# GpSimd's weight sums gated on VectorE's, oldest PSUM banks first, and one operand sum moved in an eight-core encoder block

## The chip, the cores and the metric

The kernel runs on the 8 cores of one Trainium2 chip as one program, each core on its own 1024 tokens. Nothing is exchanged between cores. The metric is the device time of one execution in microseconds, that of the slowest core. Each core has TensorE (PE, with its weight loads as PEld), VectorE (DVE), ScalarE (ACT), GpSimd (POOL) and SyncE (SP), each with an instruction queue that runs in order. They are tied together by semaphores.

## What is computed

```python
h = rms_norm(x, norm1_pre)
z = h @ w_in                              # u | v | p | gate_a | gate_b
y_a = sgu_mixer(u, v, ...)                # gMLP mixing in 128-token blocks
y_b = pool_mixer(p, w_pool, scale)        # trailing means, minus the token
merged = sigmoid(z_a) * (y_a @ w_a_out) + sigmoid(z_b) * (y_b @ w_b_out)
x = x + rms_norm(merged @ w_mix_out, norm1_post)
h = rms_norm(x, norm2_pre)
hid = silu(h @ w_gate) * (h @ w_up)
x = x + rms_norm(hid @ w_down, norm2_post)
```

## The kernel before

The whole kernel is a list of operations in program order. `S.add(engine, fn, reads, writes, after)` appends one. Each engine runs its own operations in that order, and waits only for operations of other engines that touch the same memory or stand in `after`. So the order of the Python calls is the order of every queue. The stages are A (input projection, pooling, mixing), B (gates and merge, the "gate stage"), CD (output mix, norms, FFN gate and up) and E (FFN down).

**Seven products for eight.** The gate matrices (stage B, 14 sets j) and the FFN's gate and up matrices (stage CD, 42 sets j) are multiplied by Strassen's scheme in Winograd's form (`Scheme`). A set is a 2x2 of weight quarters, loaded as `raw[j]` by a DMA that GpSimd issues, and it meets the 2x2 of activation quarters h11, h12, h21, h22. A product `prod(j, m)` is 8 matmuls of 128x128 by 128x512 into one PSUM bank. The operands of some products are sums:

- weight sums `wsums(j, part)`, L745: part 0 is s52 (128x2048) and s1 (128x1024) on VectorE, part 1 is s6 and s7 (128x1024 each) on GpSimd. Products 2 and 5 read s52, 1 reads s1, 6 reads s6, 7 reads s7;
- operand sums of the activations, `hsum`, L726 on VectorE, bf16, 4096 columns in the whole form: sums[0] or hs[0] for product 1, sums[1] or hs[1] for product 3, sums[2] or hs[2] for product 4, then h12 and h21 are overwritten by sums, for products 6 and 7.

`add2` (L721) evicts a bank on VectorE, with one input in PSUM and one in SBUF. `copy_out` (L765) evicts one on ScalarE.

**Banks.** `nb()` takes the 8 PSUM banks in rotation. It serves stage A. `balloc()` takes, of the free banks, the one with the smallest `last_use`. At the start of stage B `last_use` is -1 for all, so the first choice is bank 0, whatever stage A used last.

**The start of stage B** (L920 to L940). `gates0(0)` and `gates0(1)` are 8 banks of 16 plain matmuls each (L876), with the operands normalised beside them (L864, two SBUF inputs). `wsums(0, 0)` and `wsums(0, 1)` follow, then sums[1], then `y_part(0)`: 8 banks of 8 matmuls (L907), each evicted by `add2`, and after each pair a sum into `mergedT` (L915, two SBUF inputs). Then sums[2], sums[0], and the first `run_one_set`, which runs products 2, 5, 3, 4, 1, 6, 7 on TensorE and, through `early()`, puts s52 of set 1 and the sums for products 6 and 7 on VectorE.

**The start of the FFN** (L1104 to L1124). After the last token block's norm (L1008 on VectorE) the queue of VectorE holds: part 0 of set 0, hs[2], part 0 of set 1, the product of `d_classic(0, 0)` (L1050), three quarters of hs[0] and hs[1], the product of `d_classic(1, 0)`, half of the last block's transposed copy (L1034, `turn(7)`), the last quarters of hs[0] and hs[1], two more products, and the sums for products 6 and 7. TensorE runs `d_classic(0, 0)` and `(1, 0)` (L1062, 64 matmuls), `turn(7)` (L1027), `start(0)` and `start(1)` (products 2 and 4 of sets 0 and 1), `d_classic(0, 1)` and `(1, 1)` (64 matmuls), then `run(0)` to `run(41)` in the order 2, 3, 5, 1, 4, 6, 7. `d_classic(., 1)` needs both halves of `turn(7)`'s copy. GpSimd's `wsums(0, 1)` waits for L1008 by `after`. GpSimd's queue then has the load of `raw[2]`, and in each `run(j)` the load of set j+3 and `wsums(j + 1, 1)`.

Of the kernel before, what the change touches and what calls it, by code (L numbers as in the profile page):

```python
# [11 lines left out]
ALU = mybir.AluOpType  # L12
# [180 lines left out]
def build_program():  # L193
# [28 lines left out]
    with contextlib.ExitStack() as es:  # L222
        arena_t = es.enter_context(nc.sbuf_tensor("arena", [128, ARENA_BYTES], U8))
        psum_t = es.enter_context(nc.psum_tensor("psum", [128, 8, 512], F32))
        S = Sched(nc)
# [497 lines left out]

        def hsum(out, a_, b_, op, c0, c1):
            o, x_, y_ = out[:, :, c0:c1], a_[:, :, c0:c1], b_[:, :, c0:c1]
            S.add("dve", lambda e: e.tensor_tensor(out=o, in0=x_, in1=y_, op=op), reads=[x_, y_], writes=[o])  # L726

        class Scheme:
            def __init__(self, n, raw, ws, quads, sums, tset, load, outp):
                self.n, self.raw, self.ws, self.tset, self.load, self.outp = n, raw, ws, tset, load, outp  # L730
                (h11, h12), (h21, h22) = quads
                self.x = {1: sums[0], 2: h11, 3: sums[1], 4: sums[2], 5: h22, 6: h12, 7: h21}
                self.held = {}

            def wsums(self, j, part, which=(0, 1), after=()):
                if j >= self.n:
                    return
                r = self.raw[j % len(self.raw)]
                s52, s1, s6, s7 = self.ws[j % len(self.ws)]
                a11, a12, a21, a22 = r[:, 0, 0], r[:, 0, 1], r[:, 1, 0], r[:, 1, 1]  # L740
                jobs = (((s52, r[:, :, 0], r[:, :, 1], ALU.add), (s1, a11, a22, ALU.add)),
                        ((s6, a21, a11, ALU.subtract), (s7, a12, a22, ALU.subtract)))[part]
                for o, x_, y_, op in [jobs[i] for i in which]:
                    S.add("pool" if part else "dve",
                          lambda e, o=o, x_=x_, y_=y_, op=op: e.tensor_tensor(out=o, in0=x_, in1=y_, op=op),  # L745
                          reads=[x_, y_], writes=[o], after=after)

            def prod(self, j, m):
                r = self.raw[j % len(self.raw)]
# [89 lines left out]
        def stage_B():  # L839
# [52 lines left out]
                if d < 16:  # L892
                    dma("pool", wab_slot(d), w_ab[d])

            def y_part(p):
                t_ = (tmp[0] if p else tmp[2], tmp[1])
                for n_, i in enumerate((0, 1, 3, 2) if p < 7 else (1, 0, 2, 3)):
                    f_, hf = place[i]
                    d = 2 * p + f_
                    tk = slice(hf * HT, (hf + 1) * HT)  # L900
                    for q, src in ((0, yAT), (1, ybT)):
                        b = balloc()

                        def mmy(e, b=b, q=q, src=src, d=d, tk=tk):
                            ins = None
                            for kc in range(8):
                                ins = e.matmul(PS(b), lhsT=wab_slot(d)[:, 8 * q + kc, :], rhs=src[:, kc, tk],  # L907
                                               start=(kc == 0), stop=(kc == 7))
                            return ins
                        S.add("pe", mmy, reads=[wab_slot(d), src[:, :, tk]], writes=[PS(b)])  # L910
                        add2(t_[q][i], PS(b), t_[q][i], ALU.mult)
                        bfree(b)
                    a_, b_ = (t_[q][i].rearrange("p (t n) -> p t n", t=4) for q in range(2))
                    dstm = mergedT[:, hf * 4:(hf + 1) * 4, d, :]
                    S.add("dve", lambda e, a_=a_, b_=b_, dd=dstm: e.tensor_tensor(out=dd, in0=a_, in1=b_, op=ALU.add),  # L915
                          reads=[a_, b_], writes=[dstm])
                    if n_ >= 2:
                        wab_load(d + 2)

            wab_load(0)  # L920
            wab_load(1)
            dma("pool", wmix[0], w_mix[0])
# [2 lines left out]
            scheme.wsums(0, 0)  # L925
            scheme.wsums(0, 1)
            hsum(sums[1], h12, h22, ALU.subtract, 0, 512)
            y_part(0)
            hsum(sums[2], h21, h11, ALU.subtract, 0, 512)
            hsum(sums[0], h11, h22, ALU.add, 0, 512)  # L930

            def et2_load():
# [18 lines left out]
        def stage_CD():  # L951
# [40 lines left out]
            def c_chain(it):  # L992
# [12 lines left out]
                rstd_ops(it["ssq2"], it["rs2"], 128)  # L1005
                for i in range(2):
                    c_ = slice(i * 1024, (i + 1) * 1024)
                    it["last"] = S.add("dve", lambda e, i=i, c_=c_: e.scalar_tensor_tensor(  # L1008
                        out=it["xb"][:, c_], in0=it["xs"][:, c_], scalar=it["rs2"], in1=g2r[i],
                        op0=ALU.mult, op1=ALU.mult),  # L1010
                        reads=[it["xs"][:, c_], it["rs2"], g2r[i]], writes=[it["xb"][:, c_]])
# [7 lines left out]
            def turn(t, bank):  # L1019
                for kh in range(2):  # L1020
# [9 lines left out]
                    S.add("pe", tr, reads=[xb_, ident], writes=[PS(b)])  # L1030
                    d_ = h2q[kh][1][:, :, (t - 4) * 128:(t - 3) * 128]
                    s_ = PSB(b).rearrange("p (k n) -> p k n", k=8)
                    if kh:
                        S.add("dve", lambda e, d_=d_, s_=s_: e.tensor_copy(out=d_, in_=s_), reads=[PS(b)], writes=[d_])  # L1034
                    else:
                        S.add("act", lambda e, d_=d_, s_=s_: e.activation(out=d_, in_=s_, func=AF.Copy),
# [76 lines left out]
            scheme.start(0)  # L1113
            scheme.start(1)
            hsum(hs[1], h12, h22, ALU.subtract, 384, 512)
            hsum(hs[0], h11, h22, ALU.add, 384, 512)
            d_classic(0, 1)
            d_classic(1, 1)
            hsum(h12, h11, h12, ALU.add, 0, 512)
            hsum(h21, h21, h22, ALU.add, 0, 512)  # L1120
            scheme.wsums(0, 1, after=[items[7]["last"]])
            raw_load(2)
            for j in range(NM):
                scheme.run(j, j > 0)  # L1124
# [236 lines left out]
```

How the kernel before makes its waits and increments, by code:

```python
        def run(engname, e):  # L173
            waited = {}
            for op in per_eng.get(engname, []):
                need = {}
                for d in op.deps:
                    dop = self.ops[d]
                    if need.get(dop.sem, 0) < dop.sigval:
                        need[dop.sem] = dop.sigval
                for s, v in need.items():
                    if waited.get(s, 0) < v:
                        e.wait_ge(semh[s], v)
                        waited[s] = v
                if op.fn is None:
                    continue
                ins = op.fn(e)
                if op.signal:
                    ins.then_inc(semh[op.sem], 16 if op.dma else 1)
```

## Time and profile before

| what | value |
|---|---|
| median of 3 runs | 1499.78 us (1498.06 to 1500.7) |
| profiled execution, its own time | 1496.78 us |
| its span, slowest core (core 4) | 1495.2 us |
| spans of the eight cores | 1491.7 to 1495.2 us |
| PE busy / PEld busy | 1447.8 us (97%) / 667.4 us (45%) |
| DVE, ACT, POOL busy | 902.4, 301.3, 339.5 us |
| stage B on core 4 | 209.5 to 522 us |
| FFN gate and up, from `start(0)` | 646.2 to 1183.2 us |

The profiled execution's own time is 1.6 us above its span, and 3.0 us below the median of the runs. TensorE is the engine whose idle time counts: in most of the span one matmul follows the other. Idle time of the other engines is of interest only where TensorE waits for them.

### The profile page before, as it was taken

What the parts mean: (1) busy time and instruction counts of PE and PEld (TensorE: products, weight loads), DVE (VectorE), ACT (ScalarE), POOL (GpSimd) and SP (SyncE); (2) the same over time, 40 slices, a digit from 0 to 9 for tenths busy, and PEclk for the clock granted to TensorE, in tenths of its full rate; (3) what the DMA queues carried; (4) which work ended last, traced back from release to release, by engine and by line L of the source; (5) the groups of instructions that cost most, each with busy time, mean ns of one, the idle gap of its engine ahead of it and who ended that gap; (6) DMA issues with size and microseconds to landing.
All of it is one profiled execution on the core that took longest, in us unless ns stands there. A gap on an engine that the chain in (4) does not pass through costs nothing.

```text
span 1495.2 us, 19238 instructions; the slowest of 8 cores (1491.7 to 1495.2 us)
## 1 busy us (share of the span) xinstructions
PE 1447.8 (97%) x6827; PEld 667.4 (45%) x6962; DVE 902.4 (60%) x1185; ACT 301.3 (20%) x555; POOL 339.5 (23%) x275
## 2 busy tenths in 40 slices
PE   5999999999999999999899999999999999999997
PEld 2444444444444444444344444444444444444444
DVE  5487789666666536659887887878787500000033
ACT  4323231111111123421121212121212100000011
POOL 2100110333333100013344444444445201010100
PEclk9999999999999999999999999999999999999999
DMA  9970781565554679634355555555555858181865
GB/s 237 189 122 1 114 140 32 89 97 98 95 99 85 117 197 254 169 82 81 60 85 89 90 90 92 91 86 85 85 85 85 160 90 131 21 135 16 126 221 201
DMA packets 56685, 165.32 MB, mean 111 GB/s; under 512 B 12048, under 2 KB 14224, under 8 KB 49680
## 3 DMA queue, kind: packets, MB, share of 16 engines
q0 software_dynamic: 39792, 116.14, 48.4%
q1 hardware_dynamic: 16224, 47.32, 9.9%
q8 instruction: 58, 0.95, 0.3%
q10 hardware_dynamic: 576, 0.62, 0.1%
q14 instruction: 35, 0.29, 0.1%
HBM read 261.32 MB, written 16.78 MB: 186 GB/s over the span
## 4 chain that ended last, share of the span: by engine, by line
PE 93%; DMA 3%; DVE 2%; issue 2%; SPq 0%; DVEq 0%; ACT 0%; ACTq 0%; POOLq 0%
PE psum L758 43%; PE psum L1154 20%; PE psum L907 7%; PE psum L978 7%; PE psum L571 4%; PE psum L625 4%; PE psum L1062 2%; PE psum L876 2%; PE psum L480 2%; DMA arena<-xT 1%; DMA arena<-w_pA 1%; DVE arena L726 1%; PE psum L1198 1%; PE psum L453 0%; SPq L275 0%
## 5 line engine op out<-in xcount | busy, mean ns | idle before, releaser
L758 PE MATMUL psum<-arena 128*128 128x512 bf16 x3072 | 679.8, 381 | 13.7 <-DVE arena L726 5.7
L758 PEld LDWEIGHTS psum<-arena 128*128 128x128 bf16 x3136 | 307.5, 98 | 384.6 <-issue 19.0
L721 DVE TENSOR_TENSOR arena<-psum,arena 128x512 f32<-128x512 f32 x520 | 336.0, 684 | 179.0 <-PE psum L758 140.3
L1154 PE MATMUL psum<-arena 128*128 128x512 bf16 x1337 | 293.1, 379 | 1.4
L745 POOL TENSOR_TENSOR arena<-arena 128x1024 bf16<-128x1024 bf16 x112 | 243.0, 2192 | 55.8 <-PE psum L758 44.9
L1154 PEld LDWEIGHTS psum<-arena 128*128 128x128 bf16 x1364 | 133.5, 98 | 160.9
L1169 DVE TENSOR_TENSOR arena<-psum,arena 128x512 f32<-128x512 f32 x31 | 21.4, 692 | 249.3 <-ACT arena L1166 216.9
L765 ACT ACTIVATE arena<-psum 128x512 f32<-128x512 f32 x112 | 66.2, 596 | 379.6 <-PE psum L758 211.6
L745 DVE TENSOR_TENSOR arena<-arena 128x2048 bf16<-128x2048 bf16 x112 | 135.8, 1244 | 0.0
L1050 DVE TENSOR_TENSOR arena<-arena 128x512 bf16<-128x512 f32 x84 | 119.0, 1416 | 9.1 <-DVE arena L721 0.7
L1046 POOL DMA_DIRECT2D arena<-w_gp x42 | 32.7, 780 | 361.0 <-PE psum L758 269.1
L907 PE MATMUL psum<-arena 128*128 128x512 bf16 x502 | 111.3, 379 | 0.5
L978 PE MATMUL psum<-arena 128*128 128x512 bf16 x501 | 110.3, 379 | 0.6
L1083 ACT ACTIVATE arena<-arena 128x512 f32<-128x512 f32 x84 | 52.1, 630 | 127.6 <-DVE arena L721 127.4
L907 PEld LDWEIGHTS psum<-arena 128*128 128x128 bf16 x512 | 50.1, 98 | 60.4
L978 PEld LDWEIGHTS psum<-arena 128*128 128x128 bf16 x512 | 50.0, 98 | 59.9
L275 POOL DMA_DIRECT2D arena<-w_dn x44 | 23.4, 533 | 223.3 <-PE psum L1154 204.5
L1166 ACT ACTIVATE arena<-psum 128x512 bf16<-128x512 f32 x31 | 18.5, 597 | 268.0 <-PE psum L1154 265.9
L855 ACT ACTIVATE arena<-arena 128x512 f32<-128x512 f32 x56 | 34.4, 630 | 118.8 <-DVE arena L721 118.8
L625 PE MATMUL psum<-arena 128*128 128x512 bf16 x250 | 56.9, 379 | 0.3
L571 PE MATMUL psum<-arena 128*128 128x512 bf16 x250 | 55.3, 379 | 0.3
L453 PE MATMUL psum<-arena 128*128 128x512 bf16 x126 | 32.0, 404 | 19.7 <-DMA arena<-w_pA 15.7
(119 smaller groups left out, 746.4 us busy)
## 6 DMA issues: line engine op xcount, KB each, us to landing
arena<-w_gp POOLq DMA_DIRECT2D x42, 1024.0 KB, 9.5
arena<-w_dn POOLq DMA_DIRECT2D x44, 512.0 KB, 7.0
arena<-w_gg POOLq DMA_DIRECT2D x16, 1024.0 KB, 9.8
arena<-xT SPq DMA_DIRECT2D x16, 520.0 KB, 20.6
arena<-w_ab POOLq DMA_DIRECT2D x16, 512.0 KB, 6.7
arena<-x_ext SPq DMA_DIRECT2D x8, 1024.0 KB, 10.0
x<-arena SPq DMA_DIRECT2D x8, 1024.0 KB, 9.0
arena<-x SPq DMA_DIRECT2D x8, 1024.0 KB, 7.6
```

The costliest lines, as they stand in the source:

```text
L571: ins = e.matmul(PS(b), lhsT=hT[:, kc, tb * 128:(tb + 1) * 128], rhs=Wv[:, ct, kc, :], start=(kc == 0), stop=(kc == 15))
L625: ins = e.matmul(PS(b1), lhsT=slot[:, kc, :], rhs=hT[:, kc, hf * HT:(hf + 1) * HT], start=(kc == 0), stop=(kc == 15))
L721: S.add("dve", lambda e: e.tensor_tensor(out=out, in0=ps, in1=other, op=op), reads=[ps, other], writes=[out])
L745: lambda e, o=o, x_=x_, y_=y_, op=op: e.tensor_tensor(out=o, in0=x_, in1=y_, op=op),
L758: ins = e.matmul(PS(b), lhsT=w_[:, kc * 128:(kc + 1) * 128], rhs=x_[:, kc, :], start=(kc == 0), stop=(kc == 7))
L765: S.add("act", lambda e: e.activation(out=out, in_=PS(b), func=AF.Copy), reads=[PS(b)], writes=[out])
L855: S.add("act", lambda e: e.activation(out=o, in_=src, func=AF.Sigmoid), reads=[src], writes=[o])
L907: ins = e.matmul(PS(b), lhsT=wab_slot(d)[:, 8 * q + kc, :], rhs=src[:, kc, tk], start=(kc == 0), stop=(kc == 7))
L978: ins = e.matmul(PS(b), lhsT=mergedT[:, t, kc, :], rhs=wmix[et][:, kc, :], start=(kc == 0), stop=(kc == 15))
L1050: S.add("dve", lambda e: e.tensor_tensor(out=dst, in0=a_.rearrange("p (t n) -> p t n", t=4), in1=b_.rearrange("p (t n) -> p t n", t=4), op ...
L1083: S.add("act", lambda e: e.activation(out=o, in_=o, func=AF.Silu), reads=[o], writes=[o])
L1154: ins = e.matmul(PS(banks[t]), lhsT=hid[t // 4][:, t % 4, fc, :], rhs=slot[:, fl, :], start=(fc == 0), stop=(fc == NFC - 1))
```

## The change

Four edits, all in stages B and CD:

1. **Gate.** `wsums` of part 1 (GpSimd) now waits for the last VectorE sum of part 0 of the same set (`self.gate[j]`). For FFN set 0 the gate is the last quarter of hs[0], and for FFN set 1 it is the sum for product 7. The old `after=[items[7]["last"]]` is gone.
2. **Banks.** At the start of stage B `last_use` is set from stage A's rotation, so `balloc()` takes the oldest bank first.
3. **Operand sum.** sums[2] moves from behind `y_part(0)` to its middle, after the second L915.
4. **Copy.** For the last token block the second half of the transposed copy is done by ScalarE instead of VectorE.

```diff
+                    op_ = S.add("pool" if part else "dve",
+                                lambda e, o=o, x_=x_, y_=y_, op=op: e.tensor_tensor(out=o, in0=x_, in1=y_, op=op),
+                                reads=[x_, y_], writes=[o], after=self.gate.get(j, ()) if part else ())
+                    if not part:
+                        self.gate[j] = [op_]
...
-            def y_part(p):
+            def y_part(p, mid=None):
...
+                    if n_ == 1 and mid:
+                        mid()
...
+            for i in range(8):
+                last_use[(bank_ctr[0] + i) % 8] = i - 8
             wab_load(0)
...
-            y_part(0)
-            hsum(sums[2], h21, h11, ALU.subtract, 0, 512)
+            y_part(0, lambda: hsum(sums[2], h21, h11, ALU.subtract, 0, 512))
             hsum(sums[0], h11, h22, ALU.add, 0, 512)
...
-                    if kh:
+                    if kh and t < 7:
...
             hsum(hs[1], h12, h22, ALU.subtract, 384, 512)
-            hsum(hs[0], h11, h22, ALU.add, 384, 512)
+            scheme.gate[0] = [hsum(hs[0], h11, h22, ALU.add, 384, 512)]
...
             hsum(h12, h11, h12, ALU.add, 0, 512)
-            hsum(h21, h21, h22, ALU.add, 0, 512)
-            scheme.wsums(0, 1, after=[items[7]["last"]])
+            scheme.gate[1] = [hsum(h21, h21, h22, ALU.add, 0, 512)]
+            scheme.wsums(0, 1)
```

In the rows below each line is one instruction or a run of equal ones, in the order of the engine's queue, with the source line, the operation, its operands and its shape.

VectorE at the start of the gate stage, before: the four L721 pairs with L915 are `y_part(0)`, the L726 x2 behind them are sums[2] and sums[0].

```order
197 L726 TENSOR_TENSOR arena<-arena 128x4096
198 L721 TENSOR_TENSOR arena<-psum,arena 128x512 x2
199 L915 TENSOR_TENSOR arena<-arena 128x4x128
200 L721 TENSOR_TENSOR arena<-psum,arena 128x512 x2
201 L915 TENSOR_TENSOR arena<-arena 128x4x128
202 L721 TENSOR_TENSOR arena<-psum,arena 128x512 x2
203 L915 TENSOR_TENSOR arena<-arena 128x4x128
204 L721 TENSOR_TENSOR arena<-psum,arena 128x512 x2
205 L915 TENSOR_TENSOR arena<-arena 128x4x128
206 L726 TENSOR_TENSOR arena<-arena 128x4096 x2
207 L745 TENSOR_TENSOR arena<-arena 128x2048
```

The same place in the changed kernel (L919 is the old L915, L747 the old L745).

```order
197 L726 TENSOR_TENSOR arena<-arena 128x4096
198 L721 TENSOR_TENSOR arena<-psum,arena 128x512 x2
199 L919 TENSOR_TENSOR arena<-arena 128x4x128
200 L721 TENSOR_TENSOR arena<-psum,arena 128x512 x2
201 L919 TENSOR_TENSOR arena<-arena 128x4x128
202 L726 TENSOR_TENSOR arena<-arena 128x4096
203 L721 TENSOR_TENSOR arena<-psum,arena 128x512 x2
204 L919 TENSOR_TENSOR arena<-arena 128x4x128
205 L721 TENSOR_TENSOR arena<-psum,arena 128x512 x2
206 L919 TENSOR_TENSOR arena<-arena 128x4x128
207 L726 TENSOR_TENSOR arena<-arena 128x4096
```

One of the two 4096-column sums has moved up past two `add2` pairs and two merges.

GpSimd at the start of the FFN, before, with the semaphores that each instruction waits for (s42 is VectorE's, s44 TensorE's, s51 ScalarE's):

```order
99 L1046 DMA arena<-w_gp 128x4x1024 [waits s44]
100 L745 TENSOR_TENSOR arena<-arena 128x1024 [waits s18,s39,s42]
101 L745 TENSOR_TENSOR arena<-arena 128x1024 [waits s38]
102 L1046 DMA arena<-w_gp 128x4x1024
103 L1046 DMA arena<-w_gp 128x4x1024 [waits s42,s51,s44]
104 L745 TENSOR_TENSOR arena<-arena 128x1024 [waits s26]
105 L745 TENSOR_TENSOR arena<-arena 128x1024
```

And in the changed kernel:

```order
99 L1053 DMA arena<-w_gp 128x4x1024 [waits s44]
100 L747 TENSOR_TENSOR arena<-arena 128x1024 [waits s18,s39,s42]
101 L747 TENSOR_TENSOR arena<-arena 128x1024 [waits s38]
102 L1053 DMA arena<-w_gp 128x4x1024
103 L1053 DMA arena<-w_gp 128x4x1024 [waits s51,s44]
104 L747 TENSOR_TENSOR arena<-arena 128x1024 [waits s26,s42]
105 L747 TENSOR_TENSOR arena<-arena 128x1024
```

No instruction has moved on GpSimd. Its sums of set 1 now wait for VectorE, and those of set 0 wait for a later value of the same semaphore. The load of `raw[2]` (row 102) stands behind them.

## Rows read from the trace of the kernel before

**Rows 1.** The page, section 1: busy us, share of the span, instructions.

```profile
PE 1447.8 (97%) x6827; PEld 667.4 (45%) x6962; DVE 902.4 (60%) x1185; ACT 301.3 (20%) x555; POOL 339.5 (23%) x275
```

**Rows 2.** Waits of TensorE: us in total, times, longest.

```profile
PE psum L758 <- DVE arena L726: 5.7, 4, 2.7
PE psum L758 <- DVE arena L745: 4.5, 1, 4.5
```

**Rows 3.** The chain in order of time: start us, us, what.

```profile
759.35 10.74 PE psum L758 x49
...
1169.43 10.74 PE psum L758 x49
```

**Rows 4.** Timeline, TensorE, FFN: start, us, engine, line, operation, count [idle before].

```profile
646.21 1.45 PEld L758 LDWEIGHTS psum<-arena 128*128 128x128 bf16 x8
...
656.78 13.97 PE L1062 MATMUL psum<-arena 128*128 128x512 bf16 x63 [1.53 <-DVE arena L1034]
...
1183.25 6.79 PEld L1154 LDWEIGHTS psum<-arena 128*128 128x128 bf16 x32
```

**Rows 5.** Timeline, DVE, POOL and ACT at the FFN's start.

```profile
641.89 3.75 DVE L745 TENSOR_TENSOR arena<-arena 128x2048 bf16<-128x2048 bf16 x2
642.12 5.49 POOL L745 TENSOR_TENSOR arena<-arena 128x1024 bf16<-128x1024 bf16 x2 [10.01 <-DVE arena L1008]
...
645.56 4.20 DVE L726 TENSOR_TENSOR arena<-arena 128x4096 bf16<-128x4096 bf16 x1
...
652.20 0.60 ACT L1067 ACTIVATE arena<-psum 128x512 f32<-128x512 f32 x1 [11.16 <-DVE arena L1050]
652.69 1.02 ACT L1036 ACTIVATE arena<-psum 128x1024 bf16<-128x1024 bf16 x1
```

**Rows 6.** Timeline, at the first full FFN set, 671 to 685 us.

```profile
671.47 8.68 DVE L726 TENSOR_TENSOR arena<-arena 128x4096 bf16<-128x4096 bf16 x2
673.03 0.74 POOL L1046 DMA_DIRECT2D arena<-w_gp  x1 [24.69 <-PE psum L758]
673.79 4.20 POOL L745 TENSOR_TENSOR arena<-arena 128x1024 bf16<-128x1024 bf16 x2
...
680.08 4.86 DVE L721 TENSOR_TENSOR arena<-psum,arena 128x512 f32<-128x512 f32 x8
680.37 0.77 PEld L758 LDWEIGHTS psum<-arena 128*128 128x128 bf16 x5 [3.20 <-issue]
```

**Rows 7.** Timeline, TensorE, five sets later.

```profile
733.46 2.72 PE L758 MATMUL psum<-arena 128*128 128x512 bf16 x6 [4.54 <-DVE arena L745]
```

**Rows 8.** Windows: us, busy (x) of PE, PEld, DVE, ACT, POOL; PEclk, DMA, GB/s.

```profile
733.00:740.00 7.00, 6.32 (x17) 2.48 (x19) 5.11 (x9) 2.94 (x5) 0.00 (x0) 0.56 0.30 57
```

**Rows 9.** Timeline, the first gate bank.

```profile
209.51 27.32 PEld L876 LDWEIGHTS psum<-arena 128*128 128x128 bf16 x128 [1.23 <-issue]
...
209.97 4.66 DVE L864 TENSOR_TENSOR arena<-arena 128x512 bf16<-128x512 bf16 x1
```

**Rows 10.** Timeline, TensorE and DVE after `y_part(0)`.

```profile
250.98 8.80 PE L758 MATMUL psum<-arena 128*128 128x512 bf16 x39
...
252.66 4.49 DVE L726 TENSOR_TENSOR arena<-arena 128x4096 bf16<-128x4096 bf16 x2
...
258.20 4.49 DVE L726 TENSOR_TENSOR arena<-arena 128x4096 bf16<-128x4096 bf16 x2
...
262.83 13.97 PE L758 MATMUL psum<-arena 128*128 128x512 bf16 x62 [0.32 <-DVE arena L726]
```

**Rows 11.** Timeline, weight sums inside stage B.

```profile
275.24 4.66 POOL L745 TENSOR_TENSOR arena<-arena 128x1024 bf16<-128x1024 bf16 x2 [2.50 <-PE psum L758]
275.94 1.97 DVE L745 TENSOR_TENSOR arena<-arena 128x1024 bf16<-128x1024 bf16 x1
```

**Rows 12.** Timeline of core 3, weight loads, FFN's first and stage E's first.

```profile
645.71 1.23 PEld L758 LDWEIGHTS psum<-arena 128*128 128x128 bf16 x7
...
1181.22 4.85 PEld L1154 LDWEIGHTS psum<-arena 128*128 128x128 bf16 x23
```

More of the change, by code:

```diff
@@ L725, in hsum @@
             o, x_, y_ = out[:, :, c0:c1], a_[:, :, c0:c1], b_[:, :, c0:c1]
-            S.add("dve", lambda e: e.tensor_tensor(out=o, in0=x_, in1=y_, op=op), reads=[x_, y_], writes=[o])
+            return S.add("dve", lambda e: e.tensor_tensor(out=o, in0=x_, in1=y_, op=op),
+                         reads=[x_, y_], writes=[o])
         class Scheme:
@@ L733, in __init__, with wsums @@
                 self.held = {}
-            def wsums(self, j, part, which=(0, 1), after=()):
+                self.gate = {}
+            def wsums(self, j, part, which=(0, 1)):
                 if j >= self.n:
@@ L743, in wsums @@
                 for o, x_, y_, op in [jobs[i] for i in which]:
-                    S.add("pool" if part else "dve",
-                          lambda e, o=o, x_=x_, y_=y_, op=op: e.tensor_tensor(out=o, in0=x_, in1=y_, op=op),
-                          reads=[x_, y_], writes=[o], after=after)
+                    op_ = S.add("pool" if part else "dve",
[3 more added lines that the diff above has]
+                        self.gate[j] = [op_]
             def prod(self, j, m):
@@ L1007, in c_chain @@
                     c_ = slice(i * 1024, (i + 1) * 1024)
-                    it["last"] = S.add("dve", lambda e, i=i, c_=c_: e.scalar_tensor_tensor(
+                    S.add("dve", lambda e, i=i, c_=c_: e.scalar_tensor_tensor(
                         out=it["xb"][:, c_], in0=it["xs"][:, c_], scalar=it["rs2"], in1=g2r[i],
```

## The prediction, made before the changed kernel was run

> **What bounds the kernel now.** I read the page first: TensorE is busy for 1447.8 of 1495.2 us [rows 1], so only its stalls can be won. Then its waits: over 10 us stand behind VectorE's sums (L726, L745) [rows 2]. Then the chain, for TensorE's pace: 38 steps of 50 matmuls (49 shown, one record missing in each) between 759.35 and 1169.43 us [rows 3], so 410.08 / 1900 = 0.2158 us for a matmul that follows another. The third view is TensorE's timeline held against that pace. From the first weight load of `start(0)` at 646.21 to the first of stage E at 1183.25 [rows 4] are 537.04 us. The matmuls between are 32 (`start`) + 64 (`d_classic`) + 42 x 56 - 32 (the sets) = 2416, which at the pace are 521.4 us. **15.6 us are lost there**, and all before 740 us, since the pace holds behind it.
>
> They are lost in four places. `start(0)`'s second product waits for hs[2], `d_classic(0, 1)` for the copy L1034 (1.53 us idle) [rows 4], product 7 of set 0 for its operand sum, with 3.20 us in which no weights are loaded [rows 6], and 4.54 us go in one wait on L745 [rows 7]. Behind the last the granted clock is 0.56 [rows 8], the lower of its two levels (1.2 GHz against 2.4) for most of 7 us: there 17 matmuls were done where the pace gives 32. Without the waits that goes too.
>
> **Why VectorE is late.** Its ops with two SBUF inputs stop while GpSimd's sums run. At 641.89 s52 and s1 took 3.75 us beside GpSimd, and hs[2] at 645.56 took 4.20 [rows 5], where two such sums take 4.49, 2.20 each from start to start [rows 10]. At 671.47 the sums for products 6 and 7 took 8.68 instead of 4.49, GpSimd's pair running inside them [rows 6]. Evictions by L721, one input in PSUM, go on at 4.86 / 8 = 0.61 each.
>
> **The change at the FFN's start (edits 1 and 4), in the trace's own time.** VectorE without GpSimd beside it: s52 and s1 641.89 to 643.6 (a 1.14 + 0.60 step), hs[2] to 645.9, part 0 of set 1 to 647.6, L1050 to 648.2, the three quarters of hs[0] and hs[1] (1.67 each) to 651.5, L1050 to 652.1, and, L1034 being gone, the last quarters to 653.3. ScalarE: its L1067 waited for the first L1050 and ran at 652.20, the copy behind it at 652.69, 1.02 us long [rows 5]. L1050 comes 3.2 us earlier, so the L1067 runs at 649.0 and two copies are done by 651.1. TensorE from 646.2: product 4 of set 0 starts at 648.2 (hs[2] 645.9), product 2 of set 1 at 649.9 (s52 647.0), `d_classic(0, 1)` at 653.4 instead of 656.78 (copies 651.1). The second copy costs ScalarE 1.0 us, under 2.3 us of cover. If the cover were gone it would cost at most that 1.0 us. `d_classic` ends at 667.2.
>
> GpSimd's sums of set 0 start at 653.4 and end 4.2 us later, while VectorE waits for `d_classic`. Behind them in GpSimd's queue stands the load of raw[2]: issued at 657.6 instead of 647.6, landing 9.5 to 10 us after (page, w_gp) at about 668. Its first reader on VectorE ran at 686.5 and moves to about 678: 10 us of cover. Then the sums for products 6 and 7: they follow L1050 at 668.1 and end at 672.6. Product 7 starts at 667.2 + 32 x 0.2158 = 674.1. No stall, 1.5 us of margin. GpSimd's sums of set 1 start behind that, at 672.6, and meet only eight L721, which they do not stop. VectorE's backlog, which began with eight L721 at 680.08 [rows 6] while product 3 was done at 672.3 (7.8 us late), begins at 672.5 with product 3 done at 668.9 (3.6 us late). In the next set GpSimd waits for s1 of set 2 (679.9), so it cannot run in front of it. It then holds one L1050 for 1.4 us (682.8 to 684.2). A set gives TensorE 56 x 0.2158 = 12.1 us, VectorE needs 8 x 0.61 + 1.74, and 4 x 0.69 in every second set, so at most 9.4: the lag is gone within two or three sets, and a bank is taken again five products (8.6 us) after its use. So the wait at 733 goes as well: **-15.6 us** on core 4, from 0 (nothing goes) to 15.6 (all).
>
> In the later FFN sets the gate is idle: VectorE's part 0 stands behind product 3, GpSimd's sums behind a load that waits for product 4. Cost 0, and what hides it is that order.
>
> **The gate stage (edits 2, 3 and 1).** The first gate bank's loads start after 1.23 us without one [rows 9]. The oldest bank was last used eight rounds earlier. Of the 1.23 us, 0.1 is normal and 0.2 is regained by the next loads: **-0.9 us** (0 to 1.1).
>
> GpSimd's sums of set 0 leave 209.87, where they held a VectorE op for 4.66 us [rows 9], which nobody waited for. They go behind s1 at 239.8, beside `y_part(0)`. After it TensorE runs from 250.98, and product 7 would start at 250.98 + 48 x 0.2158 = 261.34. It starts at 262.83 [rows 10]: 1.49 us lost, because sums[2] and sums[0] (252.66, 4.49) stand ahead of s52 and the sums for products 6 and 7 (258.20, 4.49). Edit 3 takes 2.20 us out of that row and into `y_part(0)`, where VectorE has about as much idle time. But GpSimd is there now, and each L919 can be stopped. How long? In stage B the pair at 275.24 took 4.66 us for two sums of 2.12, and L745 at 275.94 took 1.97 [rows 11]: VectorE got in between the two. At 209.97 and 671.47 [rows 9, 6], with a DMA issue directly ahead of the pair, it did not. Here the semaphore wait stands ahead, as at 275.24, so I take that one: L919 runs at 244.0 and 246.7, sums[2] at 247.3, with the two w_ab issues near it (0.5 us each) that may hold it, the merge ends at 253.5 to 254, and the sum for product 7 is ready at 261.3 to 261.8. **-1.1 us** (1.5 without the w_ab issues; 0.2 if both sums go in one piece, with the sum at 262.6). The later gates in stage B make s1 0.7 us long instead of 1.97 and GpSimd 1.4 us later, with nobody waiting: 0.
>
> The Trainium skill (SBUF — State Buffer, section "SBUF: two separate sides") says that the shared port pair goes to whichever of the two engines starts first, for that whole instruction, and that the other is blocked completely. The 1.97 and 4.66 us of L745 and L864 agree on the blocking. The 4.66 us, which is two sums and not one, it does not explain. Read strictly it speaks against edit 1, since the gate only picks another loser. By it VectorE would always get in between two sums, which for this sum is the case that I took.
>
> **Sum.** Core 4: 15.6 + 0.9 + 1.1 = 17.6 us, span 1477.6. The slowest core decides. On core 3 the same stretch is 1181.22 - 645.71 = 535.5 us [rows 12], so 14.1 to win, and 2.0: 1494.8 - 16.1 = 1478.7. That is 16.5 us under the slowest span of before (1495.2). The profiled execution (1496.78) would come to 1480.3, and the median of the runs, 3.0 us above it, to **1483.3 us**.
>
> **Rivals.**
> - *Part of the backlog stays.* GpSimd's pair holds the fp32 product L1050 in odd sets in any order, and the wait at 733.46 was built up over five sets. If the lag of 3.6 us grew again instead of shrinking, that wait (4.54 us) and the slow clock behind it (about 2.9) stay: 1483.3 + 7.4 = 1490.7. Against it: after 740 us the same sets run with no loss. Chance 0.09.
> - *The gate does not do what it says.* If the stops come from something else than GpSimd's sums (weight DMAs landing, say), only the copy, the banks and the moved sum count, up to 1.5 + 0.9 + 1.1 = 3.5 us: 1496.3 to 1499. Against it: the held ops are those beside POOL rows. Chance 0.04, most of it within 0.2%.
> - *Slower.* GpSimd now waits for VectorE, its loads for GpSimd, VectorE's next s52 for the load: a loop. It decides where part 0 of a set is done more than about 8 us later than now in the FFN (there GpSimd starts some 4 us behind part 0, and s6 is needed over 8 us after its own end). If then each of 42 sets cost 0.5 us, the 21 us would more than eat the 16.5: 1504. Nothing in the steady sets comes near. Chance 0.03.
> - *Forecast*, all stalls gone but for about 1 us: 0.84.
>
> **Numbers.** Predicted 1483.3. The range must leave out no more than 2 in 10: from 1480 (core 3's stretch winning as much as core 4's, and 1.5 us of spread of runs) to 1489 (a quarter to a half of the 733 us stall left, or a new wait of some us). The 1490.7 case and beyond are left out. A measurement tells 0.2% (3 us) from no change. Faster by more than that: 0.93, within: 0.04, slower: 0.03.
>
> **What would show it.** Right: in the profile of after, no wait of TensorE on L726 or on the weight sums over 0.5 us behind 640 us; the granted clock at its upper level from 680 to 740; hs[2] 2.3 us long and the two sums for products 6 and 7 about 4.5 together; GpSimd's first FFN pair behind the last quarter of hs[0]; the first gate bank without its gap. Wrong: L745 or L1050 still 5 us long in the first five sets with TensorE waiting behind; `d_classic(0, 1)` waiting for ScalarE's second copy; a wait on the w_gp DMA; or stage B longer, with L919 held for both sums.

## The result and the profile after

The changed kernel takes 1484.55 us (median of 6 runs, the lowest 1480.58) where the kernel before took 1500.07 on the same chip. The ratio is 0.9892, interval [0.9877, 0.9906]. The prediction was 1483.3 us in a range of 1480 to 1489. Here and below the ratios and the profiles leave out runs in which the cores of a die ran at a lower clock, so a ratio can differ a little from the quotient of two medians. Ratios are always against the kernel before on the same chip.

The profiled execution took 1484.87 us, 1.6 us above the span of its slowest core (core 5). The page, busy us by engine, the same line as [rows 1]:

```profile
PE 1451.5 (98%) x6962; PEld 667.6 (45%) x6962; DVE 858.1 (58%) x1184; ACT 304.0 (20%) x556; POOL 334.4 (23%) x275
```

VectorE is busy 44 us less than in [rows 1], because its sums no longer stand still beside GpSimd's. The one instruction fewer is the copy of edit 4, which ScalarE now does. The spans of two cores, with their mean granted clock:

```profile
core 4: 1475.9 us, clock 0.999
...
core 5: 1483.3 us, clock 0.996
```

Core 4 went from 1495.2 to 1475.9. What TensorE of core 4 waits for in the changed kernel (us in total, times, longest):

```profile
PE psum L453 <- DMA arena<-w_pA: 16.2, 8, 11.4
PE psum L453 <- DVE arena L444: 1.7, 2, 1.1
PE psum L686 <- DVE arena L694: 0.4, 1, 0.4
```

Both rows of [rows 2] are gone. All that is left lies in stage A, before 206 us. Core 5 has one wait more:

```profile
PE psum L1034 <- ACT arena L992: 3.5, 1, 3.5
```

That one was not in the prediction. The experiments come back to it.

Core 4's timeline at the start of the FFN, all engines (start us, us, engine, line, operation, count, idle before). L747 is the old L745, L762 the old L758, L1069 the old L1062, L1043 ScalarE's copy, L1053 the w_gp load:

```profile
637.45 1.82 DVE L747 TENSOR_TENSOR arena<-arena 128x2048 bf16<-128x2048 bf16 x2
639.18 2.28 DVE L726 TENSOR_TENSOR arena<-arena 128x4096 bf16<-128x4096 bf16 x1
...
641.77 6.63 PEld L762 LDWEIGHTS psum<-arena 128*128 128x128 bf16 x32
...
644.39 1.94 ACT L1043 ACTIVATE arena<-psum 128x1024 bf16<-128x1024 bf16 x2
...
648.73 13.98 PE L1069 MATMUL psum<-arena 128*128 128x512 bf16 x63
649.09 4.20 POOL L747 TENSOR_TENSOR arena<-arena 128x1024 bf16<-128x1024 bf16 x2 [21.42 <-DVE arena L726]
...
662.55 67.72 PE L762 MATMUL psum<-arena 128*128 128x512 bf16 x306
663.42 4.49 DVE L726 TENSOR_TENSOR arena<-arena 128x4096 bf16<-128x4096 bf16 x2
667.83 4.87 DVE L721 TENSOR_TENSOR arena<-psum,arena 128x512 f32<-128x512 f32 x8
668.06 4.22 POOL L747 TENSOR_TENSOR arena<-arena 128x1024 bf16<-128x1024 bf16 x2 [2.33 <-DVE arena L726]
673.62 0.78 POOL L1053 DMA_DIRECT2D arena<-w_gp  x1 [1.34 <-PE psum L762]
673.85 1.82 DVE L747 TENSOR_TENSOR arena<-arena 128x2048 bf16<-128x2048 bf16 x2
675.83 4.20 POOL L747 TENSOR_TENSOR arena<-arena 128x1024 bf16<-128x1024 bf16 x2 [1.43 <-DVE arena L747]
678.76 1.83 DVE L1057 TENSOR_TENSOR arena<-arena 128x512 bf16<-128x512 f32 x1 [0.17 <-DVE arena L721]
```

Read it against [rows 5] and [rows 6]: s52 and s1 take 1.82 us instead of 3.75, hs[2] 2.28 instead of 4.20, the sums for products 6 and 7 take 4.49 instead of 8.68, and the eight evictions L721 begin 26.1 us after the stage's first weight load (667.83 - 641.77) instead of 33.9 (680.08 - 646.21). GpSimd's pair of set 0 stands where VectorE has nothing to do. Its pair of set 2, at 675.83, comes behind s1. It holds one op only, L1057 (the old L1050): 1.83 us for the usual 0.7. In 18 later sets a pair holds one L1057 too, for about 3 us (3.68 us at 703.13), and TensorE does not wait for it.

One window of core 4 (us, then busy us and instructions of PE, PEld, DVE, ACT, POOL, then PEclk, DMA share, GB/s), as [rows 8]:

```profile
680.00:740.00 60.00, 59.68 (x273) 27.18 (x278) 49.13 (x65) 12.38 (x21) 22.31 (x15) 1.00 0.48 78
```

The granted clock stays at its upper level (2.4 GHz) where it had fallen to 0.56 after the wait at 733. From the first weight load of `start(0)` at 641.77 to the first of stage E,

```profile
1163.07 7.00 PEld L1161 LDWEIGHTS psum<-arena 128*128 128x128 bf16 x33
```

are 521.30 us, where [rows 4] gave 537.04: 15.74 us less. The stretch takes 521.3 us on all eight cores. Before it took 535.0 to 537.0, so the cores win 13.7 to 15.7 us here.

The gate stage of core 4, the places of [rows 9] and [rows 10] (L880 is the old L876, L919 the old L915, L275 the issue of w_ab):

```profile
206.37 27.51 PEld L880 LDWEIGHTS psum<-arena 128*128 128x128 bf16 x128
...
237.06 6.57 POOL L747 TENSOR_TENSOR arena<-arena 128x1024 bf16<-128x1024 bf16 x2 [29.23 <-DVE arena L747]
...
240.69 0.96 DVE L919 TENSOR_TENSOR arena<-arena 128x512 bf16<-128x512 f32 x1 [0.38 <-DVE arena L721]
...
243.08 1.10 DVE L919 TENSOR_TENSOR arena<-arena 128x512 bf16<-128x512 f32 x1 [0.24 <-DVE arena L721]
243.58 1.10 POOL L275 DMA_DIRECT2D arena<-w_ab  x2
244.10 2.28 DVE L726 TENSOR_TENSOR arena<-arena 128x4096 bf16<-128x4096 bf16 x1
...
248.03 20.24 PE L762 MATMUL psum<-arena 128*128 128x512 bf16 x91
253.62 4.49 DVE L726 TENSOR_TENSOR arena<-arena 128x4096 bf16<-128x4096 bf16 x2
```

The L880 row has no idle time ahead of it, where [rows 9] had 1.23 us. TensorE runs products 2 to 7 of set 0 through from 248.03, with no wait ahead of product 6 or 7. The moved sum runs at 244.10 in its usual 2.28 us, right beside the two w_ab issues.

So the account of core 4 is 15.7 us in the FFN's start, 1.1 at the first gate bank, 1.3 between the gate stage's first weight load and the FFN's (646.21 - 209.51 = 436.70 us before, 641.77 - 206.37 = 435.40 now), 2.0 because stage A, which the change does not touch, ran that much earlier in this execution, and 0.9 given back in stage E: 19.3 in all. The 0.9 and the 2.0 are no gain of the change: the cores of this one execution reach the first gate bank anywhere from 206.37 to 208.08 us.

### The profile page after: what moved, and what is told of

It reads as the page before. It is cut to its first block, busy times and chain, and to the rows that moved or that the text cites. A ratio compares the mean times of both kernels' runs of the same rounds, so it can differ in the third digit from the quotient of the medians.

```text
span 1483.3 us, 19379 instructions; the slowest of 8 cores (1475.9 to 1483.3 us)
## 1 busy us (share of the span) xinstructions
PE 1451.5 (98%) x6962; PEld 667.6 (45%) x6962; DVE 858.1 (58%) x1184; ACT 304.0 (20%) x556; POOL 334.4 (23%) x275
## 4 chain that ended last, share of the span: by engine, by line
PE 92%; DMA 4%; DVE 1%; ACT 1%; SPq 1%; issue 0%; DVEq 0%; ACTq 0%
PE psum L762 46%; PE psum L1161 20%; PE psum L911 7%; PE psum L571 4%; PE psum L625 4%; PE psum L985 4%; PE psum L480 2%; DMA arena<-arena 2%; PE psum L1069 2%; PE psum L880 2%; DMA arena<-xT 2%; SPq L275 1%; PE psum L1205 1%; DVE arena L1005 0%; PE psum L686 0%
## 5 line engine op out<-in xcount | busy, mean ns | idle before, releaser
L762 PE MATMUL psum<-arena 128*128 128x512 bf16 x3136 | 678.3, 379 | 0.0
L762 PEld LDWEIGHTS psum<-arena 128*128 128x128 bf16 x3136 | 306.8, 98 | 369.8 <-issue 0.2
L721 DVE TENSOR_TENSOR arena<-psum,arena 128x512 f32<-128x512 f32 x520 | 336.5, 683 | 204.2 <-PE psum L762 160.9
L747 POOL TENSOR_TENSOR arena<-arena 128x1024 bf16<-128x1024 bf16 x112 | 238.1, 2148 | 129.4 <-DVE arena L747 73.1
L1057 DVE TENSOR_TENSOR arena<-arena 128x512 bf16<-128x512 f32 x84 | 116.5, 1387 | 9.0 <-DVE arena L721 0.7
L985 PE MATMUL psum<-arena 128*128 128x512 bf16 x512 | 112.8, 383 | 0.0
L1053 POOL DMA_DIRECT2D arena<-w_gp x42 | 32.7, 778 | 338.1 <-PE psum L762 268.3
L747 DVE TENSOR_TENSOR arena<-arena 128x2048 bf16<-128x2048 bf16 x112 | 102.7, 949 | 0.0
L985 PEld LDWEIGHTS psum<-arena 128*128 128x128 bf16 x512 | 50.5, 99 | 61.3 <-issue 2.4
L275 POOL DMA_DIRECT2D arena<-w_dn x44 | 23.3, 534 | 216.0 <-PE psum L1161 204.6
```

The costliest lines, as they stand in the source:

```text
L275: return S.add(eng, lambda e, o=out, i=in_: e.dma_start(out=o, in_=i), reads=[in_], writes=[out], dma=True, group=group, after=after)
L721: S.add("dve", lambda e: e.tensor_tensor(out=out, in0=ps, in1=other, op=op), reads=[ps, other], writes=[out])
L762: ins = e.matmul(PS(b), lhsT=w_[:, kc * 128:(kc + 1) * 128], rhs=x_[:, kc, :], start=(kc == 0), stop=(kc == 7))
L985: ins = e.matmul(PS(b), lhsT=mergedT[:, t, kc, :], rhs=wmix[et][:, kc, :], start=(kc == 0), stop=(kc == 15))
L1057: S.add("dve", lambda e: e.tensor_tensor(out=dst, in0=a_.rearrange("p (t n) -> p t n", t=4), in1=b_.rearrange("p (t n) -> p t n", t=4), op ...
```

## The experiments

The theory to be tested (theory A) is drawn from the prediction: the gates matter only at the start, where they stop GpSimd from holding the sums that TensorE waits for, and every later gate is idle. In its sharpest form the start is sets 0 and 1 alone. Its rival: the later gates matter too. Beside these it was open how much each of the other three edits is worth, and what the unforeseen wait of L1034 is.

**The gates alone**

```diff
-            for i in range(8):
-                last_use[(bank_ctr[0] + i) % 8] = i - 8
...
-            y_part(0, lambda: hsum(sums[2], h21, h11, ALU.subtract, 0, 512))
+            y_part(0)
+            hsum(sums[2], h21, h11, ALU.subtract, 0, 512)
...
-                    if kh and t < 7:
+                    if kh:
```

> Before, with edit 1 alone (the gate); banks, moved sum and copy as before. Theory A (VectorE's ops with two SBUF inputs are stopped beside GpSimd's sums, and these stops alone make the FFN start late): the stalls at hs[2], at product 7 of set 0 and five sets later go, and the one at L1034's copy too, since VectorE reaches it about 1 us before TensorE needs it; 15 to 15.6 us of the FFN, nothing in the gate stage or up to 0.5 us lost there: ratio 0.990 to 0.9905. Theory B (the shorter VectorE queue does it, the gate only picks who waits): under 8 us, ratio above 0.995, with the L1034 stall still there.

Measured 1483.76 us, ratio 0.9897 [0.988, 0.9913], which can't be told from the whole change (0.9892). On core 4 the gaps in the weight loads show 1.12 us lost at the first gate bank and 1.20 + 0.66 at products 6 and 7. The latter wait is there by name (waits of TensorE):

```profile
PE psum L762 <- DVE arena L726: 1.2, 2, 0.9
```

At the FFN's start nothing is lost (521.3 us from `start(0)` to stage E on every core, as in the whole change), though VectorE still does the second half of the copy (core 4, L1040 the copy, L1068 `d_classic`):

```profile
651.51 0.68 DVE L1040 COPY arena<-psum 128x1024 bf16<-128x1024 bf16 x1
...
652.59 9.66 PE L1068 MATMUL psum<-arena 128*128 128x512 bf16 x43
```

The copy is done 0.4 us before `d_classic(0, 1)` starts, and that starts on time. Edit 1 alone carries the gain of the FFN's start, and edit 4 is worth nothing beside it.

**The other three edits, without the gates** (the old wait on L1008 put back)

```diff
-                                reads=[x_, y_], writes=[o], after=self.gate.get(j, ()) if part else ())
-                    if not part:
-                        self.gate[j] = [op_]
+                                reads=[x_, y_], writes=[o], after=after if part else ())
...
-            scheme.wsums(0, 1)
+            scheme.wsums(0, 1, after=[items[7]["last"]])
```

> The changed kernel without edit 1: banks, moved sum and copy stay, GpSimd's sums start as early as before. Theory A: 0.9 us (bank) + 1.5 us (moved sum, with GpSimd out of the way) + at most 1.5 us (copy), 2.4 to 4 us in all, ratio 0.9975 to 0.9985; hs[2] again about 4.2 us long, the clock again low five sets later. Theory B: most of the 16 us stays, ratio 0.992 or less.

Measured 1494.54 us (10 runs), 0.9972 [0.996, 0.9984]: 4 us. Core 4, VectorE at the FFN's start, and TensorE's waits:

```profile
637.53 3.74 DVE L747 TENSOR_TENSOR arena<-arena 128x2048 bf16<-128x2048 bf16 x2
...
641.20 4.20 DVE L726 TENSOR_TENSOR arena<-arena 128x4096 bf16<-128x4096 bf16 x1
```

```profile
PE psum L760 <- DVE arena L747: 4.5, 1, 4.5
PE psum L760 <- DVE arena L726: 4.5, 2, 2.7
```

The lengths are those of [rows 5], and the waits those of [rows 2] less the small ones of the gate stage. Gone are the wait for L1034, the gap at the gate bank and the small waits at products 6 and 7 of the gate stage.

**The copy alone, in the kernel before**

```diff
-                    if kh:
+                    if kh and t < 7:
```

> Before, with edit 4 alone (the second half of the last block's copy on ScalarE). Theory A: the 1.5 us wait for the copy at d_classic(0, 1) goes, the wait for hs[2] (1.75 us), for product 7's sum and the one five sets later stay: 1.5 us at most. Theory B: the wait for product 7's sum shrinks as well, since VectorE has 0.7 us less to do.

One run: 1495.07 us. The wait of 1.5 us for L1034 is gone on every core. The two rows of [rows 2] stand unchanged on core 4. So the copy is worth its 1.5 us only while GpSimd makes VectorE late: edits 1 and 4 take away the same wait, and their gains don't add.

**The gates of FFN sets 0 and 1 alone** (those of the later FFN sets and of stage B left out)

```diff
-                    if not part:
-                        self.gate[j] = [op_]
```

> The changed kernel, with the gate kept only for sets 0 and 1 of the FFN; each other pair of GpSimd sums starts as early as before, and in the gate stage it does so for set 0 too. Theory A, with VectorE's lag of 3.6 us at product 3 of set 0 as the only thing that matters: set 2's s52 or s1 is stopped once for about 4 us, TensorE does not notice, and the time is that of the changed kernel, ratio 0.989 to 0.990. Rival (the gate of each set is what breaks the backlog): a wait of 2 to 4 us some sets later with the slow clock behind it, ratio 0.993 to 0.995.

Measured 1488.37 us, 0.9928 [0.9914, 0.9943], outside the interval of the gates of all sets. Theory A falls in this form. The 4.5 us wait of [rows 7] is back on every core, with a lower granted clock behind it (0.76 from 727 to 734 us on core 4). From `start(0)` to stage E the cores now take 527.4 to 528.7 us where all gates give 521.3: 6.1 to 7.4 us lost. Core 4 (L760 the products, L1055 the old L1050):

```profile
680.04 0.78 POOL L1051 DMA_DIRECT2D arena<-w_gp  x1 [1.34 <-PE psum L760]
...
680.84 4.21 POOL L747 TENSOR_TENSOR arena<-arena 128x1024 bf16<-128x1024 bf16 x2
...
694.71 6.48 DVE L747 TENSOR_TENSOR arena<-arena 128x2048 bf16<-128x2048 bf16 x2
...
707.29 5.99 DVE L747 TENSOR_TENSOR arena<-arena 128x2048 bf16<-128x2048 bf16 x2
...
719.98 5.39 DVE L1055 TENSOR_TENSOR arena<-arena 128x512 bf16<-128x512 f32 x1
...
725.89 1.81 DVE L747 TENSOR_TENSOR arena<-arena 128x2048 bf16<-128x2048 bf16 x2
...
727.24 2.25 PE L760 MATMUL psum<-arena 128*128 128x512 bf16 x6 [4.54 <-DVE arena L747]
```

GpSimd's pair of set 2 follows its load issue at once, 680.04 and then 680.84, and VectorE's s52 and s1 of the same set, begun at 680.28, take 6.46 us. The same holds in the next sets: 6.48, 5.99, 5.39. A set gives TensorE 12.1 us. VectorE needs 8 x 0.61 for its evictions, 1.74 for its weight sums, 1.4 on average for L1055, and about 4.7 for the stop: some 12.7, by this estimate. In the trace s52 starts at 680.28, 694.71, 707.29 and 725.89, which is 14.4, 12.6 and 18.6 us apart. The lag grows each time, and most in the last step, where two pairs stop VectorE, once at s1 and once at L1055. Then TensorE waits, once. By then the pair of that set has run beside L1055, so s52 and s1 take 1.81 us, VectorE is ahead again, and no further wait follows. In the kernel before it is the same: s52 and s1 take 1.81 us from 732.11 on. The prediction had 9.4 of 12.1, without a stop of s52 and s1, because it took the gate of set 2 as given.

**The gate of set 2 and none after it**

```diff
-                    if not part:
+                    if not part and self.n == 42 and j == 2:
```

> The changed kernel, gated only for sets 0, 1 and 2 of the FFN (one more gate than in start_gates). If what start_gates lost comes from GpSimd's sums starting right behind a load issue, in front of VectorE's s52 of set 2, and from a backlog that then rebuilds itself, one gate more is enough: no wait of TensorE, ratio 0.989 to 0.9905. Rival: each set's gate is needed; a wait of 4.5 us near 750 to 800 us comes back, ratio 0.993.

Measured 1482.36 us, 0.9889 [0.9874, 0.9903]. The interval overlaps those of the whole change, 0.9892 in its first measurement and 0.9872 on this chip (further down). From `start(0)` to stage E it takes 521.3 us on every core, exactly as with all gates. Its slowest core, core 4, lost 4.4 us near 598 us, in the unforeseen wait. Core 4, POOL, sets 2 and 3:

```profile
681.49 4.21 POOL L747 TENSOR_TENSOR arena<-arena 128x1024 bf16<-128x1024 bf16 x2 [1.43 <-DVE arena L747]
694.82 0.78 POOL L1053 DMA_DIRECT2D arena<-w_gp  x1 [9.12 <-PE psum L762]
695.62 4.22 POOL L747 TENSOR_TENSOR arena<-arena 128x1024 bf16<-128x1024 bf16 x2
```

In set 3 the pair again follows its load directly, without a gate, but VectorE's s52 and s1 had begun at 691.55 and were done in 1.82 us, 2.2 us before it. One gate more is enough, because VectorE is in time for all that follow. So each theory is right in part: the loop has two patterns. In one GpSimd's pair meets VectorE's sums and makes VectorE late for the next set too. It renews itself over sets 2 to 4, until TensorE has waited once. In the other VectorE is ahead, and that one lasts to the end of the stage. Which one the loop begins in is settled at the start, and set 2 belongs to the start.

**Whether a load ahead of the pair decides if VectorE gets in between** (kernel before, stage B: the next load issued directly ahead of the pair instead of behind product 4)

```diff
                 b4 = self.prod(j, 4)
-                self.load(j + len(self.raw))
...
                 b6 = self.prod(j, 6)
+                self.load(j + len(self.raw), [S.ops[-1]])
```

> Before, with one thing moved: in the 14 sets of the gate stage the load of set j+2 is issued when product 6 is done, directly ahead of GpSimd's pair, and not some 3 us earlier. If a pair that follows a load issue directly lets VectorE in only behind both sums, the s1 sums of sets 1 to 13 (L745, 128x1024), now 1.97 us beside GpSimd, take 4 us or more, and s7 takes 2.1 us instead of 2.6. If instead the kind of VectorE's op decides, they stay at 1.97. TensorE's time does not change by either.

One run, 1496.73 us, and the gate stage is as long as before: TensorE doesn't care. Core 3, the place that answers to [rows 11]:

```profile
274.17 0.57 POOL L850 DMA_DIRECT2D arena<-w_gg  x1 [7.80 <-DVE arena L721]
274.52 5.01 DVE L745 TENSOR_TENSOR arena<-arena 128x1024 bf16<-128x1024 bf16 x1
274.77 4.20 POOL L745 TENSOR_TENSOR arena<-arena 128x1024 bf16<-128x1024 bf16 x2
```

s1 took 5.01 us where it took 1.97. It began 0.25 us before the pair and still waited for both sums. It is so in sets 2 to 12 (4.4 to 5.0 us each). In set 1 the sum began during GpSimd's second one, and took 2.19 us. In set 13, which has no load ahead, it is 1.90 us, as before. By this run the op ahead of the pair decides: behind a semaphore wait VectorE gets in after the first sum, behind a load issue only after the second. The kind of VectorE's op does not decide, since the fp32 L919 above (0.96 us at 240.69) gets in as well, behind a wait.

One rival this run leaves: s1 began before the pair here, and 0.70 us after it in [rows 11], so the moment of arrival could decide. The changed kernel's own trace answers that. Core 4, a pair directly behind a load issue (701.24 to 702.02):

```profile
702.04 4.20 POOL L747 TENSOR_TENSOR arena<-arena 128x1024 bf16<-128x1024 bf16 x2
703.13 3.68 DVE L1057 TENSOR_TENSOR arena<-arena 128x512 bf16<-128x512 f32 x1
```

L1057 came 1.09 us into the first sum and still waited for both: 703.13 + 3.68 is 0.57 us, about its own work, behind the pair's end at 706.24. In the thirteen profiles of this study, on all cores, 2200 VectorE ops with two SBUF inputs were stopped by a pair behind an issue before its second sum had begun, and all 2200 waited for both sums. Behind a wait there were 728, and all got in after the first.

**The changed kernel again**

> The changed kernel once more, on the chip of the next three. Ratio 0.989. In its first profile, cores 1, 3, 5 and 7 lost 1.6 to 5.8 us near 598 us at turn(4), where TensorE waits for ScalarE, which waits for the DMA transposes of two blocks earlier; some cores will show it again, others than before if it is chance.

The ratio is 0.9872 [0.9855, 0.9889], from 1479.05, 1480.12 and 1480.42 us. The wait of L1034 near 598 us costs 1.0, 2.8, 2.4, 0.8 and 0.4 us on cores 1, 2, 5, 6 and 7. In the first profile it was cores 1, 3, 5 and 7, with 5.1, 3.5, 6.5 and 1.6. (These are the times from the first weight load of L985 to that of the last `turn(7)` bank, beyond the 127.0 us of the cores that lose nothing, so the slow clock behind the wait is counted in.) So it moves from core to core, and it sets which core is the slowest.

**The discarded squares in a place of their own** (changed kernel). L992 squares a bank for its row sum and throws the squares away, into the bf16 buffer of the block. Two blocks share that buffer, and for blocks 0 to 3 two DMA transposes (L1022) read it.

```diff
+            junkc = at(206.5 * K, K, BF16)
...
-                    junk = it["xb"][:, cols]
+                    junk = junkc
```

> The changed kernel, with the discarded output of c_mix's Square written to a 1 KB place of its own, and no more into the bf16 buffer that the DMA transposes of two blocks earlier still read. Theory: that write is what makes ScalarE, and then TensorE at turn(4), wait for the transposes; without it no core loses time near 598 us, all spans are within 1475 to 1478 us but for what a core shows elsewhere, and the time is 1480 to 1481 (ratio 0.987). Rival: the chain behind (norm of the block, which writes the same buffer) waits for the transposes just as long, the loss stays and so does the time.

Measured 1479.36 us (1478.85 to 1479.65), 0.987 [0.9857, 0.9883], with all spans between 1474.9 and 1477.3. No core loses anything near 598 us. First the changed kernel on core 5 (SPq is the DMA queue's own row, L1022 the transposes):

```profile
571.57 12.17 SPq L1022 DMA_TRANSPOSE arena<-arena  x2
...
590.73 0.60 ACT L992 ACTIVATE arena<-psum 128x512 bf16<-128x512 f32 x1 [9.53 <-DMA arena<-arena]
```

Then the same core with the squares apart (L993 the same line):

```profile
579.29 0.60 ACT L993 ACTIVATE arena<-psum 128x512 bf16<-128x512 f32 x1
```

The rows are block 2's transposes and block 4's first square. The square waits 9.53 us for the transposes to be done with a buffer of which it needs nothing. It begins 19.2 us after their issue began (590.73 - 571.57), 7 us behind the end of the queue's own row. The row shows the issuing, and what releases the square is the landing. On core 4 the same row took 8.08 us (569.95), the square ran at 582.30, 12.4 us after it began, with a wait of 2.72, and TensorE did not notice. The unforeseen wait is thus the transposes' length passed on by a shared buffer. Why they take 12 us on one core and 19 on another is open.

**The same three ways once more, on one chip:** gates with squares apart, the whole change with squares apart, and the kernel before with squares apart. The first is the gates alone with the edit just shown.

> The gate alone (as gate_only), with c_mix's discarded output in a place of its own, so that the loss near 598 us, which differs from core to core, is out of the comparison. Against junk_again it lacks the bank order, the moved sum and the copy. Its profile as gate_only lost 1.1 us at the first gate bank and 1.5 to 1.9 us at products 6 and 7 of the gate stage's first set, and nothing at d_classic(0, 1): so 2.6 to 3.0 us slower than junk_again, 1482.2 us, ratio 0.989. Rival: the copy on ScalarE is worth something by itself in the FFN's start, and the difference is over 4 us.

> The changed kernel with c_mix's discarded output in a place of its own, once more. 1479.3 us, ratio 0.987 and at most 1 us between its runs.

```diff
+            junkc = at(206.5 * K, K, BF16)
...
-                    junk = it["xb"][:, cols]
+                    junk = junkc
```

> The kernel before, with c_mix's discarded output in a place of its own. If the loss near 598 us is independent of this change, it was there before in fewer cores, and its removal takes 0 to 2 us of the slowest core: ratio 0.999 to 1.0, with the stalls at 647, 655, 677 and 728 us as before.

| kernel, squares apart | us | ratio |
|---|---|---|
| before | 1495.51 | 0.9981 [0.9971, 0.9992] |
| gates alone | 1480.38 | 0.9873 [0.9858, 0.9889] |
| whole change | 1478.12 | 0.9856 [0.9832, 0.9881] |

With the chance wait out of the way, edits 2 to 4 are worth 1480.38 - 1478.12 = 2.3 us beside the gates, and the whole change 1495.51 - 1478.12 = 17.4 us. The intervals of the last two rows overlap, so the 2.3 us rest on the traces as much as on the times. There the gap at the first gate bank is 1.12 us shorter, and from the first gate load to the first load of the output mix (L985) it is 307.35 us instead of 308.65 on all eight cores, 1.30 less: 2.4 us, all in the gate stage. What the squares apart are worth depends on where the chance wait falls. In the kernel before it is 2.8 us by the ratio. In the changed kernel it can't be told on one chip (0.987 against 0.9872), and the first profile's slowest core lost 6.5 us there.

## Why the prediction held, point by point

**What bounds it.** Right. 15.6 us were said to be lost on core 4 after 646 us, all before 740. 15.74 came back, and behind 740 us nothing changed pace. The stretch without waits was put at 521.4 us and takes 521.3, and core 3, put at 14.1, won 14.2. That gates alone give it, and no gates do not, leaves nothing for the rival by which the stops came from something else. The rival of a loop that slows itself down has no room in 521.3 us either.

**The FFN's start, edit 1.** Right, each step within 0.4 us. Counted from the first weight load of `start(0)`, us:

| step | predicted | measured |
|---|---|---|
| both copies done | 4.9 | 4.6 |
| `d_classic(0, 1)` starts | 7.2 | 7.0 |
| GpSimd's first pair | 7.2 | 7.3 |
| sums for products 6 and 7 | 21.9 | 21.7 |
| eight L721 begin | 26.3 | 26.1 |
| GpSimd's pair of set 2 | 33.7 | 34.1 |
| L1057 held beyond its 0.7 us | 1.4 | 1.1 |

**The FFN's start, edit 4.** The predicted 15.6 us were credited to edits 1 and 4 together, and that sum was right. How it is split was not said, and the experiments give the copy 0 beside the gates. The prediction moved VectorE's L1034 away and did not ask what the last quarters of hs would do with it left in: 0.68 us, under the cover that the gates had just made.

**The later FFN gates, "cost 0".** The number was right: with gates on sets 0, 1 and 2 alone the stretch is the same 521.3 us. The reason was only half. It was "VectorE's part 0 stands behind product 3, GpSimd's sums behind a load that waits for product 4". That order is the same without the gate of set 2, and there GpSimd's pair stopped s52 all the same, because VectorE was late. What makes the later gates idle is that VectorE is ahead, and this the gate of set 2 brings about. The prediction used that gate ("GpSimd waits for s1 of set 2, so it cannot run in front of it") and put no price on it: it is 6.1 to 7.4 us. The rival "part of the backlog stays" named the right mechanism and about the right price, 4.54 + 2.9 = 7.4 us. The kernel with gates on sets 0 and 1 alone is that rival, at 1488.4 against its 1490.7.

**The first gate bank, -0.9.** Right. The gap is 1.12 us shorter, and from the first gate load to `run_one_set`'s first product TensorE gives 0.2 back (41.66 us for 41.47), as predicted: 0.9.

**The moved sum, -1.1.** It gained all of the 1.49 (the 1.30 of the gate stage and the 0.2 just given back), the upper of the values given. The case chosen (VectorE gets in between the two sums) was the right one: the first L919 took 0.96 us, and the next, 1.10, met only the second sum. The term for the w_ab issues was 0.4 too much: the sum ran 2.28 us beside them. The run with the load ahead shows that the choice rested on the right row, since the pair here stands behind a wait.

On the Trainium skill's rule (SBUF — State Buffer, section "SBUF: two separate sides"), by which the shared ports are locked for one instruction: the L919 rows and s1 in set 13 agree with it. The 5.01 us beside a pair behind a load issue does not fit one instruction, and the measurement decides: there VectorE was kept out for both sums.

**The slowest core.** Wrong. Core 3 was to be the slowest, at 1478.7. It had 1480.1, and core 5 was the slowest, at 1483.3, through the L1034 wait near 598 us. That wait was in the kernel before as well, on core 7 (2.3 us) and core 6 (0.6), and the prediction read only cores 3 and 4. That 1483.3 came so close to the measured 1484.55 is luck, by two errors that cancel: the span was 4.6 us too short (1478.7 against 1483.3), and the 3.0 us that it put between the profiled execution and the median were -0.3 (1484.87 and 1484.55). With the squares apart the gain is 17.4 us, against the 17.6 of core 4's sum and the 16.5 taken from the slowest span. The terms were good. The step from one core's terms to the slowest of eight was not.

## What to carry to other kernels

Where GpSimd and VectorE both work on two SBUF inputs, let GpSimd's op wait for VectorE's last urgent one, and check the start of a loop above all: a few microseconds of lag there can renew themselves for several rounds. A round with slack on paper has none once both engines' sums meet. Of several edits aimed at one wait, ask for each what it is worth with the others in place. In a program whose time is that of the slowest core, look at the waits of every core before adding up the terms of one, and never throw an unwanted output into a buffer that somebody still reads.

## What the runs showed of the hardware that was not expected

- Two GpSimd sums of 128x1024 directly behind a load issue kept VectorE out for both: s1 took 4.4 to 5.0 us in 11 of 11 sets. Behind a semaphore wait VectorE got in after the first, 1.97 us. What in the chip makes the difference is open: that it is the op ahead was shown, why was not.
- A load issue alone cost VectorE nothing: a 4096-column sum that began while two w_ab issues (1.10 us) still ran took its usual 2.28 us.
- The same two DMA transposes of 128x1024 freed their buffer 12.4 us after their issue began on one core and 19.2 us on another, in one execution. Which other traffic does it was not tried.
